# Pooling projections moved ahead of the shift convolution, pooling sums taken in single steps among the taps of the long convolution

## The reference

```python
y_conf = conformer_conv(conf_ab, w_dw, ln_g, ln_b, w_pw)   # 31 causal taps, layer norm, silu, a matmul
y_att  = forgetting_attention(q, k, v, f_logit + b_forget) # causal softmax with a decay
y_sc   = sc_b * causal_depthwise_conv(sc_c * sc_h, w_sc)   # 3 taps ("shift convolution")
y_pool = multiscale_pool(pool_v, w_pool, pool_scale)
mix = jnp.concatenate([y_conf, y_att, y_sc, y_pool], axis=-1) @ w_out
```

## Time and profile before

| | us |
|---|---|
| median of 3 runs | 2859.71 (2854.61 to 2862.65) |
| profiled execution, its own time | 2859.21 |
| profiled execution, first to last instruction (span) | 2857.2 |
| TensorE busy | 2666.5 (93%) |
| VectorE busy | 924.3 (32%) |
| ScalarE busy | 818.3 (29%) |
| GpSimd busy | 874.5 (31%) |

### The profile page before, as it was taken

How to read it: one execution, slowest core, us unless ns; L and a number is a source line. 1 busy time by engine, 2 the same in 40 slices (tenths; PEclk the granted TensorE clock), 3 DMA queues, 4 the chain that set the end, 5 groups by cost and what they waited for, 6 DMA issues and landing times.

```text
span 2857.2 us, 30315 instructions
## 1 busy us (share of the span) xinstructions
PE 2666.5 (93%) x12580; PEld 2125.3 (74%) x12580; DVE 924.3 (32%) x1435; ACT 818.3 (29%) x1219; POOL 874.5 (31%) x492
## 2 busy tenths in 40 slices
PE   7799999999998999999998999698999999999896
PEld 4677778666686777787876777487888888888785
DVE  5213430333203544411147465504122222222423
ACT  4103441344322544422222333223211111111321
POOL 2122112444322111144632121244333332333633
PEclk8899999999998988999989999899999999999998
DMA  7001101000011000011221000120111111111111
GB/s 289 32 30 36 38 31 47 28 19 19 17 64 39 11 18 17 8 47 45 102 75 66 16 23 16 35 96 30 46 51 52 45 45 52 52 45 46 56 37 68
DMA packets 34440, 134.84 MB, mean 47 GB/s; under 512 B 3648, under 2 KB 4096, under 8 KB 32896
## 3 DMA queue, kind: packets, MB, share of 16 engines
q1 hardware_dynamic: 33984, 131.85, 13.2%
q10 hardware_dynamic: 320, 1.05, 0.1%
HBM read 123.45 MB, written 8.39 MB: 46 GB/s over the span
## 4 chain that ended last, share of the span: by engine, by line
PE 87%; DVE 6%; ACT 3%; POOL 2%; issue 2%; DMA 1%; POOLq 0%; SPq 0%; ACTq 0%; DVEq 0%
PE slot L659 55%; PE slot L705 12%; PE ps L886 4%; PE ps L857 3%; PE ps L835 2%; PE ps L737 2%; PE ps L919 1%; PE ps L910 1%; PE ps L923 1%; PE ps L936 1%; DVE ada_sum L2035 1%; DVE cacc L2098 1%; PE ps L780 1%; POOL wlo L1499 1%; DMA ada<-wada 1%
## 5 line engine op out<-in xcount | busy, mean ns | idle before, releaser
L659 PE MATMUL slot<-xhi,whi 128*128 128x512 f32 x2192 | 716.3, 409 | 57.7 <-ACT zs L1225 16.8
L659 PE MATMUL slot<-xlo,whi 128*128 128x512 f32 x2192 | 692.3, 398 | 0.0
L659 PE MATMUL slot<-xhi,wlo 128*128 128x512 f32 x2192 | 689.9, 396 | 0.0
L1499 POOL TENSOR_TENSOR wlo<-raw,whi 128x1024 fp32r<-128x1024 f32 (+1 forms) x169 | 429.4, 2541 | 829.7 <-ACT whi L1133 829.7
L659 PEld LDWEIGHTS slot<-xhi,whi 128*128 128x128 f32 x2192 | 406.4, 194 | 147.0 <-issue 65.6
L659 PEld LDWEIGHTS slot<-xlo,whi 128*128 128x128 f32 x2192 | 421.6, 192 | 92.4
L659 PEld LDWEIGHTS slot<-xhi,wlo 128*128 128x128 f32 x2192 | 420.8, 192 | 92.1
L1133 ACT ACTIVATE whi<-raw 128x1024 fp32r<-128x1024 f32 (+1 forms) x169 | 186.1, 1101 | 320.2 <-PE slot L705 174.3
L705 PE MATMUL slot<-uhi,whi 128*128 128x512 f32 x512 | 158.3, 390 | 0.0
L705 PE MATMUL slot<-ulo,whi 128*128 128x512 f32 x512 | 157.8, 389 | 0.0
L705 PE MATMUL slot<-uhi,wlo 128*128 128x512 f32 x512 | 157.6, 389 | 0.0
(11 more groups left out here) (315 smaller groups left out, 3062.2 us busy)
## 6 DMA issues: line engine op xcount, KB each, us to landing
raw<-wstream SPq DMA_DIRECT2D x129, 512.0 KB, 3.2
raw<-wstream SPq DMA_DIRECT2D x40, 640.0 KB, 3.9
ada<-wada SPq DMA_DIRECT2D x7, 1024.0 KB, 19.8
mm<-xT SPq DMA_DIRECT2D x2, 2048.0 KB, 9.7
ada<-wada SPq DMA_DIRECT2D x2, 2048.0 KB, 27.1
mm<-xT SPq DMA_DIRECT2D x8, 512.0 KB, 5.1
res_dram<-mm SPq DMA_DIRECT2D x8, 512.0 KB, 3.0
res<-res_dram SPq DMA_DIRECT2D x8, 512.0 KB, 6.5
```

The lines of the kernel that those rows point to most:

```text
L659: o = mm_(outs[:, half * HALF:(half + 1) * HALF], w[b % 2][:, k_w, :], x[:, k_x, half * HALF:(half + 1) * HALF], start=first and j == 0, s ...
L1499: tt(flat(wlo[b % 2])[:, 0:n], (raw1 if b == 1 else raw)[:, 0:n], flat(whi[b % 2])[:, 0:n].bitcast(F32), ALU.subtract).then_inc(w_lo, 1)
```

## The change

The blocks p0 and p1 go ahead of sh0; sc1 and sb1 become the last two blocks, among which the `conf` events now stand. Pooling for the first half still begins with GpSimd's two window sums, now into `wsum` and `zs[0]`. VectorE's pooling work is taken out of the evacuations of Ep0 and Ep1 and cut into eight events: `("pool", 0, 4)` and `("pool", 0, 5)` are the mean steps of the first half, `("pool", 1, 0)` to `(1, 3)` the window sums of the second and `(1, 4)`, `(1, 5)` its mean steps. They alternate with the taps that remain after Ep1. Means are written in place, into `sx` and `su`, and `ply` is gone. The shift convolution multiplies in place, in `zs[1]` for the first half and `zs[0]` for the second; Esh1's copy waits for the last mean step (`pl_done`). The forget row `ct` moves into a part of the table that is no longer read.

```diff
-    for name in NPROJ["E"] + ["sh0", "sc0", "sb0", "sh1", "sc1", "sb1", "p0", "p1"]:
+    for name in NPROJ["E"] + ["p0", "p1", "sh0", "sc0", "sb0", "sh1", "sc1", "sb1"]:
...
-    proj = proj_events("E") + dense_part_events("E" + n for n in ("sh0", "sc0", "sb0", "sh1", "sc1", "sb1"))
+    proj = proj_events("E") + dense_part_events("E" + n for n in ("p0", "p1", "sh0", "sc0", "sb0", "sh1"))
...
+    pooled = rest.index(("dense", INDEX["Ep1"], PARTS["F"] - 1)) + 1
+    late = conv[NTAPS_EARLY:]
+    ahead = len(late) * pooled // len(rest)
+    pool = [("pool", 0, 4), ("pool", 0, 5)] + [("pool", 1, step) for step in range(6)]
+    behind = [ev for pair_ in itertools.zip_longest(pool, late[ahead:]) for ev in pair_ if ev]
...
-    tl += proj[:after] + [("x1",)] + proj[after:taps] + spread(proj[taps:soft], conv[:NTAPS_EARLY]) + spread(rest, conv[NTAPS_EARLY:])
-    tl += spread(dense_part_events(["Ep0", "Ep1"])[:-2], [("conf", n) for n in range(5)])
-    tl += dense_part_events(["Ep1"])[-2:]
+    tl += proj[:after] + [("x1",)] + proj[after:taps] + spread(proj[taps:soft], conv[:NTAPS_EARLY])
+    tl += spread(rest[:pooled], late[:ahead]) + spread(rest[pooled:], behind)
+    tl += spread(dense_part_events(["Esc1", "Esb1"])[:-2], [("conf", n) for n in range(5)])
+    tl += dense_part_events(["Esb1"])[-2:]
...
                     if name == "Esh1":
-                        wait_evacuated(act, "Esc0")
-                    z, f = (zs[0], ACT.Sigmoid) if name[1] == "c" else (zs[1], ACT.Copy)
+                        act.wait_ge(pl_done, 2)
+                    z, f = (zs[0], ACT.Sigmoid) if name[1] == "c" else (zs[name == "Esh0"], ACT.Copy)
...
                 wait_evacuated(pool, "Ep0")
-                wait_evacuated(pool, "Esc1")
                 wait_evacuated(pool, "Eca1")
...
-                    if t:
-                        dve.wait_ge(sc_done, 1)
-                    v.tensor_tensor(su[:], slot[g % 2][:], zs[1][:], ALU.mult).then_inc(slot_free[g % 2], 1)
+                    su_ = zs[1 - t]
+                    v.tensor_tensor(su_[:], slot[g % 2][:], su_[:], ALU.mult).then_inc(slot_free[g % 2], 1)
...
+            def pooled(t, step):
+
+                src = (sx, su)[t]
+                if step < 4:
+                    if step == 0:
+                        dve.wait_ge(pl_done, 1)
+                        wait_evacuated(dve, "Ep1")
+                    sh = 1 << step
+                    z, src = windows[step % 2], windows[(step + 1) % 2] if step else src
+                    link(v.tensor_copy(z[:, 0:sh], src[:, 0:sh]))
+                    link(v.tensor_tensor(z[:, sh:S], src[:, sh:S], src[:, 0:S - sh], ALU.add))
+                    return
+                if (t, step) == (0, 4):
+                    dve.wait_ge(pl_in, 1)
+                r0 = DH * (step - 4)
+                rr, z = slice(r0, r0 + DH), windows[step - 4]
+                link(v.scalar_tensor_tensor(out=src[rr, 16:S], in0=z[rr, 16:S], scalar=t_("invw", t, 1)[rr, :],
+                                            in1=src[rr, 16:S], op0=ALU.mult, op1=ALU.subtract))
+                link(v.tensor_tensor(z[rr, 0:16], z[rr, 0:16], t_("invc", 16 * t, 16)[rr, :], ALU.mult))
+                ins = v.tensor_tensor(src[rr, 0:16], z[rr, 0:16], src[rr, 0:16], ALU.subtract)
+                if r0:
+                    ins.then_inc(pl_done, 1)
+                else:
+                    link(ins)
```

More of the change, by code:

```diff
@@ L1 @@
+import itertools
 from contextlib import ExitStack
@@ L377, in build @@
         cb = at("cb", 121, [P, S])
-        ct = at("ct", 125, [P, S])
+        wsum = at("wsum", 125, [P, S])
         cu = at("cu", 129, [P, 2, S])
@@ L412, in build @@
         scy = at("scy", 72, [P, 2, S])
-        ply = at("ply", 80, [P, 2, S])
         khif = at("khif", 80, [P, S], F32R)
@@ L543, in build @@
         wide_row = t_("dist")
-        LAST_USE = {1: last_tile(INDEX["Am7"]), 2: last_tile(INDEX["o7"]), 3: last_tile(INDEX["Ep1"]),
+        ct = tab[:, TABLES["strict"][0]:TABLES["strict"][0] + S]
+        windows = (wsum, zs[0])
+        LAST_USE = {1: last_tile(INDEX["Am7"]), 2: last_tile(INDEX["o7"]), 3: last_tile(INDEX["Esb1"]),
                     4: last_tile(INDEX["x7"]), 5: last_tile(INDEX["u%d_%d" % (NEIGHTH - 1, UPS - 1)])}
@@ L561, in build @@
         mix_sources = [(4, scy[:, 0, :]), (5, scy[:, 1, :]), (0, cu[:, 0, :]), (1, cu[:, 1, :]),
-                       (2, pbuf[0][:]), (3, pbuf[1][:]), (6, ply[:, 0, :]), (7, ply[:, 1, :])]
+                       (2, pbuf[0][:]), (3, pbuf[1][:]), (6, sx[:]), (7, su[:])]
         def query_ids(u, first, count):
@@ L1117, in _ @@
                         for half in range(2):
-                            o = mm_(psb[half], wpls[:, t, :], ply[:, t, half * HALF:(half + 1) * HALF],
+                            o = mm_(psb[half], wpls[:, t, :], (sx, su)[t][:, half * HALF:(half + 1) * HALF],
                                     start=True, stop=True)
@@ L1257, in evacuate @@
                     wait_tile(act, g)
-                    if name == "Ep1":
-                        wait_evacuated(act, "Esb1")
                     nc.scalar.activation((sx if name == "Ep0" else su)[:], slot[g % 2][:], ACT.Copy
@@ L1537, in window_sums @@
                     sh = 1 << step
-                    dst = zs[step]
+                    dst = windows[step]
                     link(nc.gpsimd.tensor_copy(dst[:, 0:sh], src[:, 0:sh]))
@@ L1736, in evacuate @@
                     wait_evacuated(dve, "Esh%d" % t)
-                    if t:
-                        dve.wait_ge(sc_done, 1)
-                    v.tensor_tensor(su[:], slot[g % 2][:], zs[1][:], ALU.mult).then_inc(slot_free[g % 2], 1)
+                    su_ = zs[1 - t]
+                    v.tensor_tensor(su_[:], slot[g % 2][:], su_[:], ALU.mult).then_inc(slot_free[g % 2], 1)
                     wait_evacuated(dve, name)
-                    link(v.tensor_scalar(scy[:, t, :], su[:], v_("sc", 3 * t + 2, 1), None, ALU.mult))
+                    link(v.tensor_scalar(scy[:, t, :], su_[:], v_("sc", 3 * t + 2, 1), None, ALU.mult))
                     for k in (1, 0):
                         sh = 2 - k
-                        link(v.scalar_tensor_tensor(out=scy[:, t, sh:S], in0=su[:, 0:S - sh],
+                        link(v.scalar_tensor_tensor(out=scy[:, t, sh:S], in0=su_[:, 0:S - sh],
                                                     scalar=v_("sc", 3 * t + k, 1), in1=scy[:, t, sh:S],
@@ L1753, in evacuate @@
                     v.tensor_copy(token[:, 0:1], token[:, 1:2]).then_inc(sc_done, 1)
[L1754 to L1779, removed]
                 elif name[0] == "u":
@@ L2086, in _ @@
                     compress(ev[1])
+                elif ev[0] == "pool":
+                    pooled(ev[1], ev[2])
                 elif ev[0] == "conv":
@@ L2187, in _ @@
                         v.tensor_copy(token[:, 0:1], token[:, 1:2]).then_inc(mix_src, 1)
-                    split_wide(3, 6, 6, ply[:, 0, :])
+                    split_wide(3, 6, 6, sx[:])
                 elif ev == ("conf", 0):
```

2 lines of the change are left out of this document (1 added, 1 removed).

## The result

The changed kernel takes 0.9934 of the time of the kernel before, 95% interval [0.9909, 0.996]; its runs are 2837.19, 2837.25 and 2842.78 us, beside a median of 2857.16 us. Timed again later, the ratio was 0.9938 [0.9921, 0.9954]. One run of the changed kernel in each of the two series (3075.94 and 3072.68 us, at a granted clock of 0.82) is left out; none of the 15 runs of the kernel before beside them was like that, and why is open. The forecast was 2843.2 us, a ratio of 0.9944 to its 2859.2.

The account below looks back on a forecast made before the run. TensorE, holding 87% of the chain, was taken as the bound, so only its waits and lower-clock work pay. Gains 4.3 + 2.5 + 10.2 = 17.0 us, cost 1.0: 2859.2 - 17.0 + 1.0 = 2843.2 us, range 2835 to 2852.

Parts of the forecast that it names:

- First wait: TensorE's 4.31 us stand before the second pointwise matmuls (`conf 4`), behind VectorE's queued mean steps; forecast to go, gaining 4.3 us.
- The margin: VectorE's copy of `conf 3` was to end 1 us before TensorE reaches `conf 4`.
- the one blocking that the sum held: GpSimd's weight split for x0 lengthening VectorE's work on Esc1 before the copy of `conf 3`, about 2.2 us.
- `conf 4` to T: From `conf 4` to the last projection's end (T): without a stall the matmuls stay at the upper clock, gaining 2.46 us.
- Second wait: TensorE's 20.1 us stand before the second pooling matmul; restart from T + 24.2 to T + 14.0, gaining 10.2 us.
- The blocked reading: In the hand-over, GpSimd and VectorE exclude each other, lengthening VectorE's first two remainders; TensorE restarts at T + 14.0.
- the unblocked one: The other bound: no blocking between GpSimd and VectorE in the hand-over, restart at T + 11.1, kernel 2.9 us faster.
- Middle: Eight VectorE pooling steps among the taps, 1688.8 to 1782.2 us: forecast cost +1 us, between -1.8 and +8.
- The new wait: About 1 us before a value product near 1742, as Esc0's evacuation delays unit 122's output scaling.
- the allowance above these waits for a fall of the clock: In the middle, the +8 us end counted two clock falls, about 3.4 us each plus a microsecond's stall; +1 was taken.
- Rival 1: No blocking at the end and the old small waits in the middle vanish: 2837.5 us, chance 0.15.
- Rivals 2 and 3: VectorE late at `conf 4` or clock falls mid-stretch: 2847 to 2852, chance 0.2; VectorE bounds softmax units: slower, chance 0.05.

Follow-up runs that it names:

- scale_first: Changed kernel with VectorE's `mix` list reordered: two PSUM copies, then the first pooling product's scaling, ahead of the remainders; 2830.49 us, later 2830.89 us.
- one_go: Changed kernel with all eight pooling steps in one go behind Ep1 instead of alternating with taps; 2852.64 us.

## Why the prediction was right

The second pair of traces, without the fall between `conf 0` and `conf 3`, gives its terms one by one (places are those of the first pair, which shows the same):

- First wait: `conf 3` to `conf 4` went from 12.00 to 7.52 us, 4.5 where 4.3 was the term. The margin was 1.3 us, not 1; the one blocking that the sum held (2.2 us) came as 1.97.
- `conf 4` to T: 10.00 to 7.54 us, 2.5 as forecast. The run with the mean steps moved gives the same two terms together, 6.9.
- Second wait: T + 24.2 became T + 13.3, 10.95 us where 10.2 was the term. The blocked reading held and not the unblocked one (T + 11.1): remainders of 2.13 and 3.36 us. It is 0.7 us early. About half of that is GpSimd's weight split, which took 2.38 us and not the 2.74 that the sum took from the earlier trace rows, so that the first remainder ended at T + 4.9 and not T + 5.25; the rest is small change in the steps behind.
- The rule of the Trainium skill (SBUF — State Buffer, Who interferes with whom), that a VectorE instruction with two SBUF inputs and a GpSimd one that reads SBUF exclude each other, agrees with the trace. In scale_first the copies out of PSUM and the scaling ran at 1.22 and 1.28 us beside a busy GpSimd, and only the remainders were stretched. One row that the prediction counted for the rule is of another kind: the copy of 2 elements (2.21 us) has one SBUF input.
- Middle: +0.2 us (broadcast to `conf 0`, 172.5 and 172.7), where the term was +1. The new wait stands where it was named, at 1736.24 behind Esc0's evacuation, 1.03 us. Behind Esc0's old place two waits of 0.89 us are gone, one for a value product and one for GpSimd's query remainder, as the prediction had it. What it did not have is that the other wait for a query remainder grew from 0.56 to 1.43 us (1742.89), so the middle comes out even. The term that was mis-sized is the allowance above these waits for a fall of the clock: the granted clock stayed at 0.96. VectorE's 65 us came as 65.45.

17.7 us measured against 16.0 forecast: 0.75 from the second wait, 0.8 from the middle, 0.2 from the first. In the first trace the stretch shows 16.2, nearly the forecast, but that nearness is luck: the fall between `conf 0` and `conf 3`, for which the sum has no term, took 1.6 us back. The profiled 2837.19 us lies 6.0 below the forecast; 4.8 of that lie ahead of the broadcast, where two executions of one kernel differ by as much (5.2 us before, 6.0 after).

Rival 1 named 2837.5 us, and that it is so near is luck too, for neither of its halves came about: new waits made up for the old ones (+0.2 us, not -1.8), and the blocking came. Rivals 2 and 3 did not come about: the one new fall of the clock stands behind the middle and cost 1.6 us, not 4 to 9. one_go shows what VectorE arriving late looks like: the wait that decides is one behind a block of steps, not VectorE's busy share.

## What to carry to other kernels

Work that one engine owes to nobody soon should be put between the demands of the critical engine in small steps; in one piece the same 12.8 us cost 10 us of wait, in eight pieces 0.2 us. When a wait shrinks but stays, list what stands in the releasing engine's queue ahead of the releaser and ask for each whether the waiting engine needs it: here three of the five steps ahead of it could go behind, and moving them was worth another 8.8 us of the stretch, where unblocking two of them gained 0.3. Compare two traces between landmarks around the change, not by their spans, and look for falls of the clock between the landmarks too.

## What the runs showed of the hardware that was not expected

- Holding GpSimd back until VectorE was through with its first two remainders did not remove their mutual blocking: the third remainder took 3.25 us instead of the first two taking 2.13 and 3.36.
- The same four pooling matmuls took 3.75 us after a wait of 9 us (granted clock 0.50 over them) and 1.95 after one of 1.5 (granted clock 1.00), and the first pair of dense matmuls behind them 1.5 to 1.8 against 0.84.
- Two executions of one kernel reached unit 104's broadcast up to 6 us apart (1609.31 and 1615.31 in the changed kernel), with the difference between 1000 and 1120 us and ahead of it, where the granted clock falls at other places: from 1060 to 1080 us it was 1.00 in one execution of the changed kernel and 0.75 in the other (1.00 and 0.74 in the kernel before, each time 1.00 where the broadcast came early).
- One fall of the clock (granted 0.64 over 4.7 us, worth 1.6 us) stood at the same three pairs of matmuls in five of the nine traces with the new order of blocks; the changed kernel itself had it in one trace and not in the other (granted 1.00 there).
